# Head values projected with the tokens stationary and 384 weight columns moving, instead of being turned afterwards

## What is computed

```python
z = u @ w_in[l]
(a_q, a_k, a_v, b_q, b_k, b_v, b_f, c_q, c_k, c_v, g) = jnp.split(z, split_idx, axis=-1)
o_a = _diff_attention(a_q, a_k, a_v, ...)        # 4 heads of two score maps, values 128 wide
o_b = _forgetting_attention(b_q, b_k, b_v, ...)  # 8 heads, values 64 wide
o_c = _stick_breaking_attention(c_q, c_k, c_v)   # 8 heads, values 64 wide
```

## Time and profile before

| | us |
|---|---|
| median of 3 runs | 2437.34 (2437.05 to 2437.37) |
| the profiled execution, whole | 2437.91 |
| its span, first to last instruction | 2436.1 |
| PE busy | 2426.0 |
| DVE busy | 2129.7 |
| ACT busy | 1493.0 |
| one tile of the heads in steady state | 71.5 |

### The profile page before, as it was taken

One profiled execution on the slowest core, in us unless ns is written; L12 is line 12 of the kernel. 1 busy time (PEld: TensorE's weight loads), 2 busy tenths in 40 slices (PEclk: granted clock), 3 DMA queues, 4 the chain that ended last, 5 costly groups with the idle time before them and its releaser, 6 DMA issues.

```text
span 2436.1 us, 48109 instructions
## 1 busy us (share of the span) xinstructions
PE 2426.0 (100%) x15514; PEld 2211.0 (91%) x15514; DVE 2129.7 (87%) x3960; ACT 1493.0 (61%) x2917; POOL 4.0 (0%) x14
## 2 busy tenths in 40 slices
PE   9999999999999999999999999999999999999999
PEld 8999888888899889998889998888888998899988
DVE  8999878999898779998699997789998986899985
ACT  6666457887754456664366664578786554566643
POOL 0000000000000000000000000000000000000000
PEclk9999999999999999999999999999999999999999
DMA  4333322212232323333333323321212333233332
GB/s 162 113 104 104 113 96 69 74 58 78 62 113 78 113 87 104 105 106 118 102 102 108 103 95 105 103 79 61 72 60 70 105 105 104 87 106 105 117 113 78
DMA packets 64676, 233.72 MB, mean 96 GB/s; under 512 B 7168, under 2 KB 7552, under 8 KB 64512
## 3 DMA queue, kind: packets, MB, share of 16 engines
q1 hardware_dynamic: 64368, 231.58, 29.1%
q10 hardware_dynamic: 144, 0.10, 0.0%
HBM read 229.55 MB, written 2.10 MB: 95 GB/s over the span
## 4 chain that ended last, share of the span: by engine, by line
PE 96%; DVE 2%; ACT 1%; DMA 1%; issue 0%; SPq 0%; DVEq 0%; ACTq 0%
PE ps L715 30%; PE ps L717 30%; PE ps L716 30%; PE ps L988 2%; PE ps L1031 1%; PE ps L978 1%; PE ps L979 1%; PE ps L1030 1%; DMA w_raw<-weights 1%; DVE w_lo L1997 0%; PE ps L994 0%; PE ps L1042 0%; PE ps L1043 0%; ACT w_hi L1293 0%; PE ps L962 0%
## 5 line engine op out<-in xcount | busy, mean ns | idle before, releaser
L1293 ACT ACTIVATE w_hi<-w_raw 128x512 fp32r<-128x512 f32 (+1 forms) x874 | 622.3, 721 | 475.4 <-PE ps L717 226.6
L1997 DVE TENSOR_TENSOR w_lo<-w_raw,w_hi 128x512 fp32r<-128x512 f32 (+1 forms) x874 | 699.1, 805 | 105.5 <-ACT w_hi L1293 88.9
L715 PE MATMUL ps<-u_hi,w_hi 128*128 128x256 f32 (+1 forms) x2432 | 786.0, 323 | 0.9 <-DVE w_lo L1997 0.9
L717 PE MATMUL ps<-u_hi,w_lo 128*128 128x256 f32 (+1 forms) x2432 | 781.1, 321 | 0.0
L716 PE MATMUL ps<-u_lo,w_hi 128*128 128x256 f32 (+1 forms) x2432 | 780.2, 321 | 0.0
L716 PE MATMUL ps<-area,w_hi 128*128 128x256 f32 (+1 forms) x1778 | 583.4, 328 | 0.0
L715 PEld LDWEIGHTS ps<-u_hi,w_hi 128*128 128x128 f32 x2432 | 463.3, 190 | 37.4 <-issue 2.4
L717 PEld LDWEIGHTS ps<-u_hi,w_lo 128*128 128x128 f32 x2432 | 463.2, 190 | 35.1
L716 PEld LDWEIGHTS ps<-u_lo,w_hi 128*128 128x128 f32 x2432 | 463.4, 191 | 32.9
L715 PE MATMUL ps<-area,w_hi 128*128 128x512 f32 (+1 forms) x1414 | 482.0, 341 | 1.0 <-ACT scratch_whole L1392 0.9
L717 PE MATMUL ps<-area,w_lo 128*128 128x512 f32 (+1 forms) x1414 | 480.1, 340 | 0.0
(11 more groups left out here) (220 smaller groups left out, 2909.9 us busy)
## 6 DMA issues: line engine op xcount, KB each, us to landing
w_raw<-weights SPq DMA_DIRECT2D x432, 512.0 KB, 3.7
h<-x SPq DMA_DIRECT2D x4, 512.0 KB, 6.8
out<-scratch_whole SPq DMA_DIRECT2D x8, 256.0 KB, 2.0
scratch_whole<-const_b SPq DMA_DIRECT2D x1, 512.0 KB, 10.1
scratch_whole<-const_r SPq DMA_DIRECT2D x1, 192.0 KB, 9.2
cst<-const SPq DMA_DIRECT2D x1, 137.0 KB, 8.6
par<-params ACTq DMA_DIRECT2D x1, 98.0 KB, 4.9
```

Of the source, the lines that this page charges most:

```text
L715: pe.matmul(dst, hi, x_hi, start=start, stop=False, **kw)
L717: return pe.matmul(dst, lo, x_hi, start=False, stop=stop, **kw)
L1293: return act.activation(dst, src, ACT.Copy)
L1997: return dve.tensor_tensor(dst, src, hi_part.bitcast(F32), ALU.subtract)
```

## The change

The three value units of a tile are taken together. The host packs their columns so that for each of the 8 blocks of the contraction the values of a, b and c stand side by side, 384 columns. They move, and 128 tokens of `u` stand still: `value_steps` runs 32 steps, (block k, token block j), each of three matmuls of 384 columns, in two passes: tokens 0 and 1, then 2 and 3. Where the 384 columns run over the end of the ring of slots (k = 2), a step has three matmuls of 256 columns and three of 128. The result has tokens on partitions, so the twelve value transposes of a tile go. As the norm factor is now one per partition, PE turns `rstd` once per layer (`turn_rstd`, four transposes). ACT and DVE split the values straight from PSUM, per token block, scaling by that factor. The three `take` of the values go. The values live in the area in which the head outputs come to lie later.

The order changes: per tile the units are now c queries, c keys, the value steps, b queries, b keys, a queries, a keys (before: the a values were last). On DVE the a queries' `take` stands behind the four `turned_lo`, right before the a keys' `take`; the four `rows` (bias rows) of a tile stand together; `split(1)` stands ahead of `output_lo` and `differences` in `rest_of_tile`.

```diff
+            def value_steps(begin, end, before):
+                for n in range(begin, end):
+                    late, m = divmod(n, 2 * UNIT)
+                    k, j = m // 2, 2 * late + m % 2
+                    if n == 0:
+                        pe.wait_ge(staged, c.next(staged, 2 if before else 1))
+                    elif n == 2 * UNIT:
+                        pe.wait_ge(staged, c.next(staged))
+                    elif n == 2 * UNIT + 1 and before:
+                        pe.wait_ge(v_set, c.next(v_set))
...
+                    columns = ((0, 2), (2, 3)) if k == 2 else ((0, 3),)
+                    for x, w, part in ((x_hi, w_hi, 0), (x_lo, w_hi, 1), (x_hi, w_lo, 2)):
+                        for first, after in columns:
+                            b = (2 * UNIT + 3 * k + first) % (SLOTS * UNIT)
+                            last = pe.matmul(ps[:, val_banks(before)[j], first * P:after * P], x, w[:, b * P:(b + after - first) * P],
+                                             start=k == part == 0, stop=k == UNIT - 1 and part == 2, skip_group_check=True)
...
+            def turn_rstd():
                 for j in range(NQ):
-                    last = pe.transpose(ps[:, AUX, j * P:(j + 1) * P], tile(st)[:, j * P:(j + 1) * P], ident)
+                    last = pe.transpose(ps[:, SB0, j * P:(j + 1) * P], rstd[:, j * P:(j + 1) * P], ident)
...
+                unit(own[1], 0)
                 turn_probs(0)
+                unit(own[2], 1, 0, 6)
+                weighted(t, 2, 1)
+                scores(1, 0)
+                unit(own[2], 1, 6)
+                bank_read(1 if before else 2)
+                unit(own[3], 2, 0, 4)
                 turn_probs(0)
+                unit(own[3], 2, 4)
+                weighted(t, 1, 0)
                 scores(1, 1)
...
(ACT, end of a tile)
                 turned_hi(3)
-                values_hi(1)
-                qk_hi(0, 0, 6, 2)
-                qk_hi(0, 2, 7)
+                qk_hi(0, 0, 0)
+                qk_hi(0, 2, 1)
                 exps(1, 0)
...
(DVE, end of a tile)
                 turned_lo(3)
-                values_lo(1)
-                take(7, 1.0)
-                qk_lo(0, 0, 6)
-                take(8, 1.0)
+                take(0, banks[2], SCALE)
+                take(1, banks[3], 1.0)
                 block_max(1, 0)
                 block_max(1, 1)
                 block_max(1, 2)
-                qk_lo(0, 2, 7)
+                qk_lo(0, 0, 0)
                 block_max(1, 3)
+                qk_lo(0, 2, 1)
                 output_lo(2, t)
                 share_out(1, 0, prob_set)
...
(DVE, values)
+                dve.scalar_tensor_tensor(val_block(t, 0, 1, j), of[:, 0:P], scale, val_block(t, 0, 0, j).bitcast(F32),
+                                         ALU.mult, ALU.subtract)
+                dve.scalar_tensor_tensor(val_parts(t, j, 1), of[:, P:3 * P].rearrange("p (b n) -> p b n", n=HEAD), scale,
+                                         val_parts(t, j, 0).bitcast(F32), ALU.mult, ALU.subtract).then_inc(v_set, 1)
```

More of the change, by code:

```diff
@@ L1048, in diff_norm, with unit @@
                 pe.matmul(ps[:, bank, :], ones_r[:], o_sq_lo, start=False, stop=True).then_inc(o_ms, 1)
[L1050 to L1055, removed]
+            def unit(bank, k, first_block=0, end=UNIT, first=False):
+                last = u_unit(bank, k, (first_block, end), first)
@@ L1116, in heads @@
-                weighted(1, 0)
+                else:
+                    pe.wait_ge(v_set, c.next(v_set, 2))
+                own = (AUX, 0, 1, AUX) if before else (0, AUX, 1, AUX)
+                unit(own[0], 2, 0, 5)
+                weighted(t, 2, 0, before)
+                stick_scores(1)
+                unit(own[0], 2, 5)
+                unit(own[1], 0)
+                turn_probs(0)
+                unit(own[2], 1, 0, 6)
+                weighted(t, 2, 1)
+                scores(1, 0)
@@ L1122, in mixer @@
             def mixer():
[L1123 to L1136, removed]
+                heads(0, False)
+                for t in range(1, NT):
+                    heads(t, True)
+                rest_of_tile(NT - 1, unit)
+                bank_read()
+                unit(2, 2, 0, 7)
                 turn_probs(0)
-                gate(2, 7)
+                unit(2, 2, 7)
                 pe.wait_ge(o_set, c.peek(o_set, 3 * NT - 2))
@@ L1719, in heads @@
                 stick_sigmoids(3)
+                if not before:
+                    values_hi(t, 0, before)
+                    values_hi(t, 1, before)
                 split(2)
@@ L2506, in sums_of_forget, with take @@
                 dve.wait_ge(vec_done, c.next(vec_done))
[L2508 to L2514, removed]
+            def take(k, bank, scale, first=False):
+                if not first:
                     dve.wait_ge(qk_set, c.peek(qk_set, 0))
                 dve.wait_ge(unit_done, c.next(unit_done))
[L2517 to L2522, removed]
+                dve.scalar_tensor_tensor(tile(k), ps[:, bank, :], scale, rstd[:], ALU.mult, ALU.mult).then_inc(staged, 1)
             def qk_lo(branch, which, k):
@@ L2620, in output_lo @@
             def output_lo(branch, t):
[L2621 removed]
+                rounded, rest = (area[:, o_at(branch, t, part):o_at(branch, t + 1, part)] for part in range(2))
                 src = o_whole[:]
@@ L2718, in heads @@
                 turned_lo(3)
-                take(6, SCALE)
+                split(2)
+                qk_lo(1, 2, 1)
                 split(0)
```

259 lines of the change are left out of this document (133 added, 126 removed).

## The result

| | before | after |
|---|---|---|
| median of 11 runs, us | 2437.19 (2436.88 to 2437.93) | 2443.26 (2442.88 to 2443.38) |
| span of the profiled execution | 2436.1 | 2441.1 |

The change makes the kernel slower by 6.1 us: 1.0024 of the time before, 95% interval 1.0016 to 1.0032. The prediction had 2443.0 and a range of 2436 to 2457.

What follows compares the result with a forecast made beforehand. PE's work was taken to bound the heads. Matmuls and transposes -1.2, turning rstd +0.9 and the wait +6.0 summed to +5.7 us, a median of 2443.0; own bounds 2440 to 2447, range 2436 to 2457.

Steps and rivals of the forecast that it cites:

- value products and transposes: PE's value steps: new matmuls of 384, 256 and 128 columns against removed matmuls and transposes, -0.15 a tile, -1.2 us.
- turning `rstd`: Four added PE transposes per layer, 2 x 0.44 = +0.9 us; the wait for ACT's copy stands over 5.8 us later.
- wait ahead of `turn_probs(1)`: Tile end: PE waits for DVE's last share of branch b, head 1; 0.75 a tile, +6.0 us, bounds 3 and 10.
- wait of `weighted(1, 1)`: PE behind DVE's evictions at the tile end; moved bias rows repay the lost air: 0, at most 0.2 a tile.
- The narrow product: Value steps at k = 2: a float32r matmul of 128 columns, not in the trace, taken as 0.12 us.
- The bound that I drew from the records of 2 columns: PE records of 2 columns behind weight loads 0.11 apart: with 128 stationary columns a record costs 0.11 however little moves.
- The first: Rival: narrow products done like full fp32, 0.22 each, 9.6 us more, 2452.6; chance 0.33, with or without the wait.
- the third rival: Narrow products cost by their columns, 0.066: 5.2 us less, 2437.8 with the wait, 2431.8 without; chance 0.08.
- The chain: Tile end, from head 0's transposes: turned_lo, take, ACT's eight copies, subtractions, output_lo, shares; ends at 12.2 against 11.55 due.
- The second rival: The 0.65 wait is absent because the a queries' take gets in earlier: 2437.0; chance 0.14.
- ACT's string: Tile end: after the copies, three exponentials, copy of weights, fourth exponential, out at 11.4; DVE reaches the fourth share at 11.5.
- The cover that I put at nothing: Evictions, slots, splits and value waits taken as covered, at no cost; without cover each a wait up to 1.2 us a tile.

Runs made afterwards that it cites:

- the two edits: Against the changed kernel (2443.26): a queries' take ahead of the four turned_lo, 2439.99; output_lo(2) moved to DVE's idle stretch, 2442.12; both together, 2436.36.

## Why the prediction was right, point by point

**The forecast held**: slower, by the wait that it named. Its sum against what the trace shows, in us:

| term | predicted | found |
|---|---|---|
| value products and transposes | -1.2 | -2.6 |
| turning `rstd` | +0.9 | +0.9 |
| wait ahead of `turn_probs(1)` | +6.0 | +6.6 |
| wait of `weighted(1, 1)` | 0 | 0 |
| scores of branch b, head 0 | 0 | +1.8 |
| `turn_probs(0)` at the end of a layer | 0 | +0.6 |
| wait of the next tile's first unit, before | 0 | -0.8 |
| sum | +5.7 | +6.5 |

Matched instruction by instruction, PE's two stretches of heads are 3.27 and 3.26 us longer than before, 6.5, so the sum holds there. Outside them the two profiled executions differ by -1.5: -0.4 in the first 39 us and -1.1 between the layers, most of it two waits, 0.7 together, at 1565 and 1567 us that only the one before has. The profiled execution before was 0.7 above its median and that of after was at its own; whether the change has a part in the rest stays open. That the median came out within 0.3 of the forecast is luck in part: terms that were off by 0.6 to 1.8, two of them below the forecast and three above, nearly cancel.

- **The narrow product** was mis-sized by a little: 0.109, not 0.12. With 0.1745 for the 384 columns, taken as 0.175, that makes the -2.6: 84 x 0.1745 + 12 x 0.2285 = 17.40 a tile, against 17.73 removed. The bound that I drew from the records of 2 columns was the value itself. (What the products carry above their columns at 2.4 GHz is 13 to 15 ns, not 13 to 14.) The first and the third rival fall with the runs of 384 and of 320 and 64 columns. The Trainium skill (TensorE: Matmul & The Clock Gate, section LDWEIGHTS) gives a weight load its columns over 1.2 GHz, 107 ns for 128 (an estimate from that page), and the 0.109 agrees. Its section Back-to-back issue gap has about 56 ns for 128 moving columns alone and about 81 in a stream of loads and products; the measured 0.109 is above both.
- **The wait** was 0.83, forecast 0.75 (0.65 by the chain). The chain was right: counted from the end of head 0's transposes (487.56), the last share is out at 12.25 (499.81), forecast 12.2, and the last group was due at 11.52 (498.43 + 0.65), forecast 11.55. That is 0.73; the 0.1 above it are the hand-over to PE and its start from rest. The second rival falls: 2437.0 needed the wait to be absent. ACT's string was in the working too, 0.1 ahead of DVE's. What the working lacked is DVE's own string from the first score on, which now holds the a queries' subtractions and which the run with the take first laid bare at 0.45. Neither of the two edits alone takes the wait away.
- **The cover that I put at nothing and that wasn't there** is that of the b keys' rests. I had checked slots, splits and value evictions, and not the place that the b keys' rests have: in the new order PE comes to the scores of head 0 right after `weighted(2, 1)`, and there is no unit between. It is the step that failed, at 1.8 us.
- **A wait of before that I did not see**: in each tile the first unit of the next tile came 0.10 late behind the scores. Its product starts at 420.24 and the next at 420.57, 0.33 apart instead of 0.23; by the program it waits for a staging tile, and DVE's take of the a values lasted to 420.10. That take is one of the three that went, and after has none of this wait; no run separates it.

```profile
420.24 0.49 PE L715 MATMUL ps<-u_hi,w_hi 128*128 128x512 f32 x1
420.57 0.40 PE L716 MATMUL ps<-u_lo,w_hi 128*128 128x512 f32 x1
```

- **DVE** should have been 1.5 us less busy per tile; it was 4.2 us less in all, 0.5 a tile. The three takes went as worked out (24 fewer, 17 us), but the eight value subtractions cost 0.34 for 128 columns and 0.47 for 256, 3.3 a tile, and the five that they replace had cost 2.2 (40 instructions, 17.4). Added up, DVE's instructions are 8.9 us shorter (2345.1 to 2336.2); its busy time, which counts instructions that overlap once, fell by 4.2.

## What to carry to other kernels

A wait on the later of two strings is shortened only as far as the other string is shorter; work out both from the same zero, and move what nobody needs there out of each. An operation that is dropped from the bound engine moves every due time behind it forward, and the engines that feed it need that much air. When the operand's packing makes narrow products, pack it anew: 128 columns cost no less than 0.11 here, and 64 columns as much.

## What the runs showed of the hardware

- A float32r product with 128 stationary columns takes 0.11 us whether 128 or 64 columns move (a pair with 256 takes 0.2285, a pair of 320 and 64 takes 0.257). Records of unrounded fp32 with 2 moving columns stand behind loads 0.11 apart as well. From 256 columns on a float32r product is 13 to 15 ns above its columns at 2.4 GHz (384: 0.1745).
- A moving operand of three blocks with a stride of eight blocks costs the same 0.174 as a contiguous one of 384 columns.
- The list of PE's waits doesn't hold the wait of 0.83 a tile, in total the largest of PE's (6.6 us; the list's first entry is 3.3). It lies in three pieces of 0.25 to 0.31 between groups of transposes whose modelled ends reach over them. In the run with `output_lo` moved, where it is one piece, the list has it:

```profile
PE ps L1004 <- DVE scratch_whole L2583: 3.8, 8, 0.5
```

The distance between starts shows it in both. The Trainium skill (Perfetto Trace Analysis, section Tensor Engine Instruction) says that the end of a tensor instruction is estimated from its size, and the rows here agree: ten transposes show 1.25 of busy time where the next unit begins 1.01 after them.
